# The layout of three bf16 parts that a gather by matmul reads, in a mixture-of-experts kernel

## The chip, the cores and the metric

One core of one Trainium2 chip runs the whole program. The metric is the device time of one execution in microseconds (us); lower is better. The time before is the median of 3 runs, 1986.92 us (1986.51 to 1989.77). One further execution was profiled; all rows come from it.

## What is computed

A two-part encoder layer on 256 tokens of 2048 channels, in float32. The first part (token mixing with four branches) and the modulation vectors are not touched by the change. The second part is the one that matters:

```python
h2 = modulate(rmsnorm(x, norm2_g[l]), sh2, sc2)     # norm, then * (1 + scale) + shift per channel
pg = softmax(ht @ rg_w + rg_b); pg_top, g_idx = top_k(pg, 1)          # 1 group of 4
le = (ht @ re_w + re_b)[group]; pe_top, e_idx = top_k(softmax(le), 2) # 2 of its 8 experts
y = (silu(x_tok @ w1[e]) * (x_tok @ w3[e])) @ w2[e]  # for each token's two experts of 32
x = x + gt2 * sum_of_weighted(y);  out = rmsnorm(x, final_g)
```

Each expert has 12 MB of float32 weights (w1, w3, w2), and all 32 of them are read once.

## The kernel before

The program has one instruction stream for each engine, synchronised by counting semaphores that are written out by hand.

**The normalised input and its parts.** After the token mixing, `xn2` (in the buffer `r_b`, 128 partitions x 4096 elements, that is 2 tiles of 128 tokens with 2048 channels each) holds the normalised rows. TensorE transposes them (line 715) for the router. For the experts they are kept as three bf16 parts whose sum is the float32 value, in `xparts` (line 145): ScalarE rounds `xn2` to part 0 (line 1020), GpSimd subtracts part 0 from it in place (line 470, first instruction, which also waits until the transposes have read `r_b`), ScalarE rounds the remainder to part 1 (line 1032), and GpSimd subtracts again and writes part 2 (line 470, second instruction). All four write and read their elements in the order of memory. In ScalarE's stream line 1032 stands behind the two exponentials of the router (lines 1028 and 1030).

**The router** runs at the same time: logits on TensorE (lines 723 and 724), then a chain of small VectorE instructions (lines 1368 to 1459), each waiting for the one before, with a few matmuls between them. It ends in a table that says which expert each pass takes, and in one-hot selection matrices: `sel` (bf16, who goes where) and `selw` (with weights). `sel_e` is the piece of 64 columns for one pass.

**The pass loop.** A pass computes one expert for up to 64 tokens. `gather(half)` (line 758) builds the input of a pass, transposed: for each of 8 blocks of 128 channels it adds up six matmuls (2 token tiles x 3 parts), in which a 128-column piece of `xparts` is the stationary operand and the 64 columns of `sel_e` are the moving one; 48 matmuls in all. A channel block k is the set of channels q*16 + k, since the expert weights are loaded with 16 neighbouring channels in one partition. So the stationary operand takes every 16th bf16 element (`xparts_k`, line 146), a step of 32 bytes. VectorE scales and shifts the result (lines 1481 and 1484) into `xe`. `first(p)` (line 802) multiplies `xe` with w1 and w3, four channel blocks (one chunk c) at a time; `second` (line 780) multiplies with w2. The loads of a pass are issued by SyncE (lines 411 and 417), each when TensorE has finished with the buffer (`w13_used`, `w2_used`); there are buffers for one expert. Before the loop, `gather(0)` and `gather(1)` of pass 0 stand alone (lines 823 to 825), then come the transposes of `selw` (line 830) and `first(0)`; within `first(p)` stands `gather(0)` of the next pass, behind chunk 1, and `gather(1)` stands between `first(p-1)` and `first(p)`.

**Waits around the parts.** The gather waits for both subtractions (`parts_sub`, line 822); VectorE waits for them before it writes `selw` into `r_b` (lines 1461 and 1462). SyncE issues no load of the loop before the table is there (line 431).

Of the kernel before, what the change touches and what calls it, by code (L numbers as in the profile page):

```python
# [14 lines left out]
ALU = mybir.AluOpType  # L15
ACT = mybir.ActivationFunctionType
AX_X = mybir.AxisListType.X

P = 128
D = 2048  # L20
S = 256
KT = D // P
TT = S // P
# [44 lines left out]
def build(nc, x, c, ada_w, ada_b, norm1_g, w_in, pool_w, pool_scale, conf_dw_w, conf_dw_b, conf_ln_g,  # L68
          conf_ln_b, branch_w, sc_conv_w, w_o, norm2_g, rg_w, rg_b, re_w, re_b, exp_w1, exp_w3,
          exp_w2, final_g, keep_consts, mix_consts, iota_const, out):  # L70
    with ExitStack() as ctx:
        def sb(name, shape, dt=F32):
            return ctx.enter_context(nc.sbuf_tensor(name, shape, dt))

        def sem(name):
            return ctx.enter_context(nc.semaphore(name))
# [5 lines left out]
        r_b = sb("r_b", [P, KT * S])  # L82
# [17 lines left out]
        xn2 = r_b[:, :].rearrange("p (t d) -> p t d", t=TT)  # L100
# [22 lines left out]
        def at(name, shape, dt, offset):  # L123
            return nc.alloc_sbuf_tensor_at(name, shape, dt, offset=base + offset)
# [18 lines left out]
        xe = ring[:, 5, 0:KT * NWIN].rearrange("p (c n) -> p c n", c=KT)  # L143
        y_sb = ring[:, 5, 1024:2048].rearrange("p (b n) -> p b n", b=2)
        xparts = at("xparts", [P, 3, TT, D], BF16, 90112)
        xparts_k = xparts[:, :, :, :].rearrange("p i t (q k) -> p i t k q", k=KT)
        sel = r_c[:, 0:576].bitcast(BF16).rearrange("p (t j) -> p t j", t=TT)
        sel_e = r_c[:, 576:640].bitcast(BF16).rearrange("p (t n) -> p t n", t=TT)
        wT = r_c[:, 640:1664].rearrange("p (i t) -> p i t", i=4)
# [3 lines left out]
        selw = r_b[:, 1024:3072]  # L153
        fgrow = r_b[:, 2048:4096]
        squares = r_b[:, 0:2048]
        remain = r_b
        ident, ones, tri = keep[:, 0:128], keep[:, 128:256], keep[:, 256:384]
        io8 = keep[:, 384:400].rearrange("p (t e) -> p t e", t=TT)
        prow = ring[:, 0, 0:384].rearrange("p (a b) -> p a b", a=3)
# [20 lines left out]
        def tiles(b, n=2):  # L180

            return ps[:, b:b + n, :].rearrange("p b (h t) -> p (b h) t", t=S)
# [51 lines left out]
        h2_t = sem("h2_t")  # L234
# [30 lines left out]
        parts_sub = sem("parts_sub")  # L265
        parts_act = sem("parts_act")
# [37 lines left out]
        def y_bank(n):  # L304
            return 4 * (n % 2) + 2
# [154 lines left out]
        @block.gpsimd  # L460
        def _(pool):
            pool.dma_start(r_c[:, :], mix_consts).then_inc(mixc_in, 16)

            flat = "p t d -> p (t d)"
            for i in range(2):
                pool.wait_ge(parts_act, i + 1)
                dst = remain[:, :] if i == 0 else xparts[:, 2, :, :].rearrange(flat)
                if i == 0:
                    pool.wait_ge(h2_t, 8)
                nc.gpsimd.tensor_tensor(dst, r_b[:, :], xparts[:, i, :, :].rearrange(flat),  # L470
                                        ALU.subtract).then_inc(parts_sub, 1)


        @block.tensor
        def _(pe):
            mm = nc.tensor.matmul
# [12 lines left out]
            for b in range(8):  # L489
                for k in (2 * b, 2 * b + 1):  # L490
                    for t in range(TT):
                        last = nc.tensor.transpose(tiles(b, 1)[:, k % 2, t * P:(t + 1) * P],
                                                   x_in[:, t, k * P:(k + 1) * P], ident)
# [47 lines left out]
            for n in range(5):  # L541
# [3 lines left out]
                if n == 3:  # L545

                    pe.wait_ge(conv_done, 1)
                    for m in range(MT):
                        last = mm(ps[:, y_bank(n), 0:S], ones, brT[:, 1, m, :], start=(m == 0), stop=(m == MT - 1))
                    last.then_inc(ln_sum, 1)  # L550
                if n == 4:
                    pe.wait_ge(ln_step, 1)
                    pe.wait_ge(sc_done, 1)
                    for m in range(MT):
                        last = mm(ps[:, y_bank(n), 0:S], ones, pq[:, m, 0:S], start=(m == 0), stop=(m == MT - 1))
# [11 lines left out]
            for q in range(4):  # L567
                b = (2, 3, 6, 7)[q]
                for t in range(TT):
                    last = mm(ps[:, b, :], tmp[0][:, t * MIX + q * P:t * MIX + (q + 1) * P], dftp[:, t, :],  # L570
                              start=(t == 0), stop=(t == TT - 1))
# [4 lines left out]
            for q in range(4):  # L576
                for t in range(TT):
                    last = mm(pt[:, q, :], tmp[1][:, t * MIX + q * P:t * MIX + (q + 1) * P], pool_c[:, t, q, :],
                              start=(t == 0), stop=(t == TT - 1))
            last.then_inc(pool_done, 1)  # L580

            def gate_y(n, kts, lhs, rhs):

                y = tiles(y_bank(n))
                for f in range(4):
                    for k in range(kts):
                        last = mm(y[:, f, :], lhs(k, f), rhs(k), start=(k == 0), stop=(k == kts - 1))  # L587
                return last
# [3 lines left out]
            for q in range(4):  # L592
                mm(tiles(2)[:, q, :], dftc[:, 0:128], pq[:, q, 0:S], start=True, stop=False)
                last = mm(tiles(2)[:, q, :], dftc[:, 128:256], pq[:, q, S:2 * S], start=False, stop=True)
# [26 lines left out]
            for j in range(4):  # L621
# [15 lines left out]
                last = gate_y(n, 1, lambda k, f: pw[:, j, f * P:(f + 1) * P], lambda k: brT[:, 0, j, :])  # L637
# [3 lines left out]
            for k in range(KT):  # L641
                last = mm(ps[:, 6, k:k + 1], acc_k[:, k, :], ones[:, 0:1], start=True, stop=True)
# [28 lines left out]
            for k in range(KT):  # L671
                last = mm(ps[:, 6, k:k + 1], acc[:, k * P:(k + 1) * P], ones[:, 0:1], start=True, stop=True)
# [7 lines left out]
            def wo_products(k, t, n):  # L680
                y = 2 * k + n // 2
                hi = g_hi[y % 4][:, (n % 2) * MIX:(n % 2 + 1) * MIX]
                o = (y % 4) * 1024 + (n % 2) * MIX
                lo = g_lo[:, (WO0 + y // 4) % W_SLOTS, o:o + MIX]
                m_hi = (m_hi_a, m_hi_b)[k // 8][:, k % 8, t * P:(t + 1) * P]
                mm(ps[:, 4 * t + n, :], m_hi, hi, start=(k == 0), stop=False)  # L686
                mm(ps[:, 4 * t + n, :], m_hi, lo, start=False, stop=False)  # L687
                return mm(ps[:, 4 * t + n, :], m_lo[:, k, t * P:(t + 1) * P], hi, start=False, stop=(k == KT - 1))  # L688

            for y in range(28):  # L690
# [3 lines left out]
                for t in (1, 0):  # L694
# [3 lines left out]
                    for n in (2 * (y % 2), 2 * (y % 2) + 1):  # L698
                        last = wo_products(y // 2, t, n)
                last.then_inc(g_used, 1)  # L700
            pe.wait_ge(g_lo_done, 128 + 32)
            for t in range(TT):
                for n in range(4):
                    for k in (14, 15):
                        last = wo_products(k, t, n)
# [6 lines left out]
            for b in range(8):  # L712
                for k in (2 * b, 2 * b + 1):
                    for t in range(TT):
                        last = nc.tensor.transpose(tiles(b, 1)[:, k % 2, t * P:(t + 1) * P],
                                                   xn2_k[:, t, k, :], ident)
# [10 lines left out]
            for t in range(TT):  # L727
                last = nc.tensor.transpose(ps[:, 1, t * 36:(t + 1) * 36], logitT[:, t * P:(t + 1) * P],
                                           ident[0:36, 0:36])
# [21 lines left out]
            gat = ps[:, 0, :].rearrange("p (c n) -> p c n", n=NWIN)  # L751

            def gather(half):
                for kk in range(HALF):
                    k = half * HALF + kk
                    for t in range(TT):
                        for i in range(3):
                            last = mm(gat[:, kk, :], xparts_k[:, i, t, k, :], sel_e[:, t, :],  # L758
                                      start=(t == 0 and i == 0), stop=(t == TT - 1 and i == 2))
                last.then_inc(gathered, 1)  # L760

# [31 lines left out]
            def first(p, with_second):  # L793
                for c in range(4):
                    if c % 2 == 0:
                        pe.wait_ge(xe_ready, 2 * p + c // 2 + 1)
                    for m in range(2):
                        pe.wait_ge(w13_in[2 * c + m], 16 * p + 16)
                    for kk in range(4):
                        k = 4 * c + kk  # L800
                        for m in range(2):
                            last = mm(ps[m * NWIN:(m + 1) * NWIN, 2, :], xe[:, k, :],  # L802
                                      chunk(2 * c + m)[:, kk * F:(kk + 1) * F],
                                      start=(k == 0), stop=(k == KT - 1))
                    last.then_inc(w13_used, 1)
                    if with_second and c == 0:
                        second(p, 0, 2)
                    if c == 1:
                        pe.wait_ge(sel_ready, p + 2)
                        pe.wait_ge(xe_ready, 2 * p + 2)  # L810
                        gather(0)
                        if with_second:
                            second(p, 2, 4)
                    if with_second and c == 2:
                        for b in range(2):
                            turn_output(p, b)
# [11 lines left out]
            for i in range(4):  # L828
                for t in range(TT):
                    last = nc.tensor.transpose(tiles(4)[:, i, t * P:(t + 1) * P],  # L830
                                               selw[:, t * PAIRS + i * P:t * PAIRS + (i + 1) * P], ident)
# [16 lines left out]
            for i in range(4):  # L848
# [6 lines left out]
                for k in range(KT):  # L855
                    last = nc.tensor.transpose(ps[:, b + k // 4, (k % 4) * P:(k % 4 + 1) * P],
                                               YS[:, k, i * P:(i + 1) * P], ident)
                last.then_inc(yT_done, 1)
            yn = ring[:, 0:2, :].rearrange("p s (i d) -> p (s i) d", d=D)
            for t in range(TT):  # L860
# [5 lines left out]
                for n in range(4):  # L866
                    for i in range(4):
                        last = mm(ps[:, 4 * t + n, :], wT[:, i, t * P:(t + 1) * P], yn[:, i, n * MIX:(n + 1) * MIX],  # L868
                                  start=(i == 0), stop=(i == 3))
# [4 lines left out]
        def _(act):  # L874
            A = nc.scalar.activation
# [21 lines left out]
            for t in range(TT):  # L897
                last = A(r_b[:, t * D:(t + 1) * D], x_in[:, t, :], ACT.Square, accum_out=stat[:, t:t + 1])
# [118 lines left out]

            act.wait_ge(xn2_ready, 2)
            act.wait_ge(x1_ready, 8)
            A(xparts[:, 0, :, :], xn2, ACT.Copy).then_inc(parts_act, 1)  # L1020
            for b in range(0, 8, 2):
                act.wait_ge(h2_t, b + 1)
                for k in (2 * b, 2 * b + 1):
# [5 lines left out]
            act.wait_ge(r_ask, 2)  # L1029
            A(rs[:, 8, :], rs[:, 7, :], ACT.Exp).then_inc(r_exp, 1)  # L1030
            act.wait_ge(parts_sub, 1)
            A(xparts[:, 1, :, :].rearrange("p t d -> p (t d)"), remain[:, :], ACT.Copy).then_inc(parts_act, 1)
            act.wait_ge(table_ready, 1)
            A(sel_e, sel[:, :, 0:NWIN], ACT.Copy).then_inc(sel_ready, 1)  # L1034
            act.wait_ge(selw_t, 1)
# [578 lines left out]
```

## Time and profile before

| | |
|---|---|
| median of 3 runs | 1986.92 us |
| the profiled execution's own time | 1989.88 us |
| its span, first to last instruction | 1988.1 us (1.8 us less than its time) |
| mean granted clock of TensorE | 0.951 of full |
| busy: TensorE matmul, VectorE, ScalarE, GpSimd | 91%, 37%, 21%, 1% of the span |
| instructions of the gather (line 758) | 3120 matmuls, 65 gathers of 48 |

The busy times of TensorE are modelled ends of pipelined matmuls, so the distance from one start to the next is the better measure of its pace. The profile gives for each stretch the granted clock (1.00 is 2.4 GHz, 0.50 is 1.2 GHz), the share of time in which the 16 DMA engines are busy, and the rate that they move. All positions are microseconds from the start of the span.

### The profile page before, as it was taken

How to read it: one execution, taken by the hardware profiler on the slowest of the kernel's cores; microseconds unless marked ns; L12 is line 12 of the kernel's file. 1: busy time of each engine (PE TensorE's matmuls, PEld its weight loads, DVE VectorE, ACT ScalarE, POOL GpSimd, SP SyncE). 2: the span in 40 equal slices, each digit the busy share in tenths (PEclk: the TensorE clock that was granted, in tenths of full speed). 3: DMA queues.
4: the chain of work that ended last, by engine and by line, in shares of the span. 5: the costliest groups of instructions: out<-in, count | busy, mean ns of one | idle time of the engine just before them, and what ended most of it. 6: DMA issues, size and time to landing. Idle time of an engine off the chain costs nothing.

```text
span 1988.1 us, 28852 instructions
## 1 busy us (share of the span) xinstructions
PE 1815.1 (91%) x11742; PEld 1233.8 (62%) x11742; DVE 729.1 (37%) x824; ACT 424.3 (21%) x506; POOL 16.8 (1%) x7
## 2 busy tenths in 40 slices
PE   1189999999999999997399999999999999999987
PEld 1178855998999999886245454544545445445444
DVE  5848855585545634444611111111111111111113
ACT  3020003332323323334111111111111111111112
POOL 0000000000000000000300000000000000000000
PEclk8589999998999999998699999999999999999999
DMA  8998676497565644455099999999999999999971
GB/s 364 419 367 329 239 294 250 156 399 292 218 249 206 259 170 170 160 194 208 5 380 422 422 422 422 422 422 422 422 422 422 422 422 422 422 422 422 422 333 64
DMA packets 128765, 641.11 MB, mean 322 GB/s; under 512 B 12944, under 2 KB 13380, under 8 KB 64196
## 3 DMA queue, kind: packets, MB, share of 16 engines
q1 hardware_dynamic: 127568, 638.12, 79.4%
q0 software_dynamic: 144, 1.70, 0.2%
q8 instruction: 46, 0.75, 0.1%
q10 hardware_dynamic: 996, 0.44, 0.1%
q14 instruction: 11, 0.09, 0.0%
HBM read 638.14 MB, written 2.10 MB: 322 GB/s over the span
## 4 chain that ended last, share of the span: by engine, by line
PE 70%; DMA 21%; DVE 6%; issue 1%; ACT 1%; ACTq 0%; SPq 0%; DVEq 0%
DMA ring<-in_exp_w 17%; PE ps L802 16%; PE ps L523 7%; PE ps L780 7%; PE ps L758 6%; PE ps L611 5%; PE ps L613 5%; PE ps L615 5%; PE ps L587 4%; DMA ring<-in_ada_w 4%; PE ps L536 3%; DVE r_m L1119 2%; PE ps L868 1%; PE ps L686 1%; PE ps L687 1%; PE ps L688 1%
## 5 line engine op out<-in xcount | busy, mean ns | idle before, releaser
L802 PE MATMUL ps<-ring 128*64 128x512 f32 x2048 | 468.1, 599 | 8.4 <-DMA ring<-in_exp_w 5.0
L802 PEld LDWEIGHTS ps<-ring 128*64 128x64 f32 x2048 | 151.1, 137 | 270.9 <-issue 265.7
L615 PE MATMUL ps<-h_hi,g_lo 128*128 128x256 f32 x1024 | 293.6, 287 | 0.0
L1481 DVE TENSOR_TENSOR r_c<-ps,scale 128x512 f32<-128x512 f32 x65 | 44.9, 691 | 535.4 <-PE ps L758 535.2
L758 PEld LDWEIGHTS ps<-r_c,xparts 128*128 128x128 bf16 x3120 | 199.6, 168 | 58.6 <-issue 51.1
L611 PE MATMUL ps<-h_hi,mix_hi 128*128 128x256 f32 x768 | 224.5, 292 | 6.8 <-DVE g_lo L1242 3.7
L613 PE MATMUL ps<-h_lo,mix_hi 128*128 128x256 f32 x768 | 221.3, 288 | 0.0
L758 PE MATMUL ps<-r_c,xparts 128*128 128x64 bf16 x3120 | 206.6, 228 | 7.3 <-ACT r_c L1034 5.2
L615 PEld LDWEIGHTS ps<-h_hi,g_lo 128*128 128x128 f32 x1024 | 200.6, 196 | 0.0
L975 ACT ACTIVATE mix_hi<-ring 128x1024 fp32r<-128x1024 f32 x96 | 101.3, 1059 | 276.1 <-PE ps L615 263.4
L611 PEld LDWEIGHTS ps<-h_hi,mix_hi 128*128 128x128 f32 x768 | 151.8, 198 | 8.2 <-DVE g_lo L1242 4.3
L1119 DVE SCALAR_TENSOR_TENSOR r_m<-ring,ccol,r_m 128x2048 f32<-128x2048 f32 x60 | 141.1, 2352 | 39.5 <-DMA ring<-in_ada_w 37.9
L1242 DVE TENSOR_TENSOR g_lo<-ring,mix_hi 128x1024 fp32r<-128x1024 f32 x96 | 117.2, 1225 | 98.8 <-ACT mix_hi L975 96.3
L613 PEld LDWEIGHTS ps<-h_lo,mix_hi 128*128 128x128 f32 x768 | 151.7, 198 | 0.4
L523 PE MATMUL ps<-r_h,ring 128*128 128x256 f32 x640 | 140.4, 383 | 1.4 <-ACT r_h L913 1.4
L1059 ACT ACTIVATE ring<-ps 128x512 f32<-128x512 f32 x64 | 34.7, 595 | 471.5 <-PE ps L780 471.5
L523 PEld LDWEIGHTS ps<-r_h,ring 128*128 128x128 f32 x640 | 122.9, 192 | 18.4 <-issue 1.4
L780 PE MATMUL ps<-ring,r_c 128*64 128x512 f32 x512 | 119.2, 607 | 3.1 <-DVE r_c L1498 3.1
L780 PE MATMUL ps<-r_b,r_c 128*64 128x512 f32 x512 | 116.9, 598 | 0.0
L1490 DVE TENSOR_TENSOR r_m<-ps,mod 128x512 f32 x64 | 41.2, 687 | 203.0 <-PE ps L790 203.0
L587 PE MATMUL ps<-r_b,ring 128*128 (+1 forms) x416 | 94.3, 384 | 0.3 <-DVE mod L1156 0.3
L780 PEld LDWEIGHTS ps<-ring,r_c 128*64 128x64 f32 x512 | 40.8, 139 | 79.9 <-issue 79.9
(247 smaller groups left out, 1675.4 us busy)
## 6 DMA issues: line engine op xcount, KB each, us to landing
ring<-in_exp_w SPq DMA_DIRECT2D x320, 1024.0 KB, 21.1
ring<-in_w_in SPq DMA_DIRECT2D x46, 2048.0 KB, 8.9
ring<-in_ada_w SPq DMA_DIRECT2D x32, 2048.0 KB, 11.8
r_b<-in_exp_w SPq DMA_DIRECT2D x64, 1024.0 KB, 21.2
ring<-in_ada_w SPq DMA_DIRECT2D x32, 1024.0 KB, 9.0
ring<-in_w_o SPq DMA_DIRECT2D x8, 2048.0 KB, 7.6
ring<-in_branch_w SPq DMA_DIRECT2D x6, 2048.0 KB, 10.7
r_m<-in_x SPq DMA_DIRECT2D x1, 2048.0 KB, 12.9
```

Source lines behind the costliest of these rows:

```text
L523: last = mm(u[:, f, :], w[:, kk, f * P:(f + 1) * P], hT[:, k, :], start=(k == 0 and f % 2 == 0), stop=(k == KT - 1), skip_group_check=True)
L536: last = mm(ps[:, u_bank(n) + t, :], hT[:, k, t * P:(t + 1) * P], w[:, kk, :], start=(k == 0), stop=(k == KT - 1))
L587: last = mm(y[:, f, :], lhs(k, f), rhs(k), start=(k == 0), stop=(k == kts - 1))
L611: mm(u[:, f, :], hi[:, o:o + P], h_hi[:, k, :], start=(k == 0 and f % 2 == 0), stop=False, skip_group_check=True)
L613: mm(u[:, f, :], hi[:, o:o + P], h_lo[:, k, :], start=False, stop=False, skip_group_check=True)
L615: last = mm(u[:, f, :], lo[:, o:o + P], h_hi[:, k, :], start=False, stop=(k == KT - 1), skip_group_check=True)
L758: last = mm(gat[:, kk, :], xparts_k[:, i, t, k, :], sel_e[:, t, :], start=(t == 0 and i == 0), stop=(t == TT - 1 and i == 2))
L780: last = mm(ps[side * NWIN:(side + 1) * NWIN, 4 + b, :], hid[:, f, :], chunk(CHUNKS + f)[:, q * MIX:(q + 1) * MIX], start=(f == 0), stop=( ...
L802: last = mm(ps[m * NWIN:(m + 1) * NWIN, 2, :], xe[:, k, :], chunk(2 * c + m)[:, kk * F:(kk + 1) * F], start=(k == 0), stop=(k == KT - 1))
L975: A(g_hi[x % 4], slot(q % W_SLOTS)[:, (x % 4) * 1024:(x % 4 + 1) * 1024], ACT.Copy).then_inc(g_hi_done, 1)
L1119: ins = V.scalar_tensor_tensor(out=acc, in0=w[:, i, :], scalar=ccol[:, kk:kk + 1], in1=acc, op0=ALU.mult, op1=ALU.add)
L1242: V.tensor_tensor(g_lo[:, q, (x % 4) * 1024:(x % 4 + 1) * 1024], slot(q)[:, (x % 4) * 1024:(x % 4 + 1) * 1024], g_hi[x % 4].bitcast(F32), ...
```

## The change

`xparts` is kept contraction-major: within each token tile, channel q*16 + k is stored at k*128 + q. The four instructions that make the parts walk `r_b` in the order of memory, as before, and walk `xparts` with an inner step of 128 elements (256 bytes) and 16 steps, for each of 128 channels q. The gather reads 128 neighbouring elements. Nothing else is changed; number, order, waits and sizes of all instructions stay. The values computed are the same.

```diff
-        xparts_k = xparts[:, :, :, :].rearrange("p i t (q k) -> p i t k q", k=KT)
+        xparts_q = xparts[:, :, :, :].rearrange("p i t (k q) -> p i t q k", k=KT)
+        xn2_q = r_b[:, :].rearrange("p (t q k) -> p t q k", t=TT, k=KT)
...
-            flat = "p t d -> p (t d)"
-            for i in range(2):
-                pool.wait_ge(parts_act, i + 1)
-                dst = remain[:, :] if i == 0 else xparts[:, 2, :, :].rearrange(flat)
-                if i == 0:
-                    pool.wait_ge(h2_t, 8)
-                nc.gpsimd.tensor_tensor(dst, r_b[:, :], xparts[:, i, :, :].rearrange(flat),
-                                        ALU.subtract).then_inc(parts_sub, 1)
+            pool.wait_ge(parts_act, 1)
+            pool.wait_ge(h2_t, 8)
+            nc.gpsimd.tensor_tensor(xn2_q, xn2_q, xparts_q[:, 0, :, :, :], ALU.subtract).then_inc(parts_sub, 1)
+            pool.wait_ge(parts_act, 2)
+            nc.gpsimd.tensor_tensor(xparts_q[:, 2, :, :, :], xn2_q, xparts_q[:, 1, :, :, :], ALU.subtract
+                                    ).then_inc(parts_sub, 1)
...
-                            last = mm(gat[:, kk, :], xparts_k[:, i, t, k, :], sel_e[:, t, :],
+                            last = mm(gat[:, kk, :], xparts[:, i, t, k * P:(k + 1) * P], sel_e[:, t, :],
...
-            A(xparts[:, 0, :, :], xn2, ACT.Copy).then_inc(parts_act, 1)
+            A(xparts_q[:, 0, :, :, :], xn2_q, ACT.Copy).then_inc(parts_act, 1)
...
-            A(xparts[:, 1, :, :].rearrange("p t d -> p (t d)"), remain[:, :], ACT.Copy).then_inc(parts_act, 1)
+            A(xparts_q[:, 1, :, :, :], xn2_q, ACT.Copy).then_inc(parts_act, 1)
```

## Rows read from the trace of the kernel before

**Rows 1.** Windows: busy time of each engine, TensorE's clock, DMA share, GB/s.
```profile
core 0: us, PE busy (x) PEld busy (x) DVE busy (x) ACT busy (x) POOL busy (x), PEclk, DMA share, GB/s
980.00:985.00 5.00, 3.23 (x48) 3.10 (x48) 4.48 (x9) 0.31 (x1) 0.00 (x0) 0.50 0.01 3
...
994.00:1000.00 6.00, 6.00 (x16) 2.01 (x18) 0.00 (x0) 0.00 (x0) 0.00 (x0) 0.52 0.73 309
...
1012.00:1014.00 2.00, 2.00 (x10) 0.43 (x6) 0.00 (x0) 0.00 (x0) 0.00 (x0) 1.00 0.91 303
...
1022.00:1024.00 2.00, 2.00 (x12) 0.79 (x10) 0.00 (x0) 0.00 (x0) 0.00 (x0) 1.00 0.95 299
...
1024.00:1100.00 76.00, 76.00 (x530) 37.39 (x528) 11.62 (x18) 10.97 (x16) 0.00 (x0) 1.00 1.01 422
...
1500.00:1925.00 425.00, 418.38 (x2896) 206.47 (x2892) 64.00 (x100) 70.32 (x101) 0.00 (x0) 1.00 1.01 422
```
**Rows 2.** The chain that ended last: start, length, what.
```profile
944.04 7.03 PE ps L723 x32
...
961.84 6.81 DVE ct L1412
...
1057.40 3.15 PE ps L758 x48
...
1086.46 3.12 PE ps L758 x48
...
1791.14 25.43 DMA ring<-in_exp_w
...
1820.96 25.43 DMA ring<-in_exp_w
```
**Rows 3.** Timeline of the parts and the router: start, length, instruction, idle before.
```profile
938.83 3.62 ACT L1020 ACTIVATE xparts<-r_b 128x4096 bf16<-128x4096 f32 x1
...
944.20 7.94 POOL L470 TENSOR_TENSOR r_b<-r_b,xparts 128x4096 f32<-128x4096 f32 x1 [942.28 <-PE ps L715]
...
952.93 0.17 DVE L1372 TENSOR_TENSOR r<-lg,rs 128x8 f32<-128x8 f32 x1
...
956.95 3.60 ACT L1032 ACTIVATE xparts<-r_b 128x4096 bf16<-128x4096 f32 x1
...
960.63 7.93 POOL L470 TENSOR_TENSOR xparts<-r_b,xparts 128x4096 bf16<-128x4096 f32 x1 [8.49 <-ACT xparts L1032]
...
961.84 6.80 DVE L1412 TENSOR_SCALAR ct<-ct 32x128 f32<-32x128 f32 x1
```
**Rows 4.** Timeline between the table and the loop.
```profile
981.65 3.23 PE L758 MATMUL ps<-r_c,xparts 128*128 128x64 bf16 x48 [5.25 <-ACT r_c L1034]
...
985.43 0.69 DVE L1481 TENSOR_TENSOR r_c<-ps,scale 128x512 f32<-128x512 f32 x1 [0.26 <-DVE r_b L1468]
...
986.91 3.21 PE L758 MATMUL ps<-r_c,xparts 128*128 128x64 bf16 x48 [2.03 <-DVE ring L1484]
...
993.99 9.92 PE L802 MATMUL ps<-ring 128*64 128x512 f32 x32 [2.12 <-issue]
...
1000.66 21.68 SPq L411 DMA_DIRECT2D ring<-in_exp_w  x10
...
1014.02 3.18 PE L758 MATMUL ps<-r_c,xparts 128*128 128x64 bf16 x48
```
**Rows 5.** Line 758: duration in ns (least, median, most), first and last start.
```profile
L758 PE MATMUL ps<-r_c,xparts x3120: 225/227/274, 981.6 to 1912.7; 128*128 128x64 bf16 x195
```
**Rows 6.** Line 503 alone (128x128 f32 weights, one column): windows, neighbouring, then strided.
```profile
core 0: us, PE busy (x) PEld busy (x), PEclk, DMA share, GB/s
259.00:262.00 3.00, 3.00 (x29) 3.00 (x28) 1.00 1.01 374
361.00:364.00 3.00, 3.00 (x15) 3.00 (x15) 1.00 0.00 0
```

More of the change, by code:

```diff
@@ L155, in build @@
         squares = r_b[:, 0:2048]
-        remain = r_b
         ident, ones, tri = keep[:, 0:128], keep[:, 128:256], keep[:, 256:384]
```

## Prediction

> **What bounds the kernel now.** I read the windows first. From 1024 us to 1925 us the sixteen DMA engines are fully busy and move 422 GB/s in every stretch [rows 1]; this is the reading of the expert weights. Then the chain that ended last. In its first half it runs through TensorE alone, and one gather of the same kind follows the other after 1086.46 - 1057.40 = 29.06 us [rows 2]. In its second half it is a transfer of 25.43 us, once in 1820.96 - 1791.14 = 29.82 us [rows 2]. 12 MB (12.58 million bytes) at 422 GB/s are 29.8 us, so the pass is bound by the DMA, and TensorE, which could do a pass in 29.06 us, only catches up over some sixteen passes and then waits. Since the DMA is full from 1024 us on in both halves, the end of the loop is set by the moment at which the stream of loads starts again and by the bytes, not by TensorE.
>
> So the stretch that matters lies before. The DMA stands still while the router makes its table (0.01 busy at 980 to 985 us, [rows 1]); SyncE may not go on without it. The first load of the loop that waits for TensorE goes out at 1000.66 us [rows 4]. Everything on the way from the normalised rows to that point moves the end one for one. The reader is to see two things on that way. One is an instruction of VectorE on 32x128 elements that takes 6.80 us and stands in the chain that ended last [rows 2, 3]. It starts at 961.84 us, while GpSimd's second subtraction runs from 960.63 us for 7.93 us, to 968.56 us; VectorE's instruction ends at 968.64 us, 0.08 us later [rows 3]. The next starts of the router follow from there. VectorE was held until GpSimd was done. The other is the gather of pass 0, twice, at 981.65 and 986.91 us [rows 4].
>
> **The change part by part.** It moves no wait and adds no instruction; it changes how the same elements lie, and so only durations.
>
> The gather. 65 x 48 matmuls read their stationary operand as neighbours instead of with a step of 32 bytes. Before, 48 of them take 3.18 us at the full clock [rows 4], less 0.23 us for the last one's own length [rows 5], over 47: 63 ns from start to start. At half the clock it is (3.23 - 0.25) / 47 = 63 ns as well [rows 1, 4]. In the loop a saving is hidden: the DMA's 29.82 us stand against 29.06 us. Should it be halved there, TensorE waits 3 us more in each pass. It can show only before 1024 us. The first gather of pass 0 ends at 984.88 us, but the VectorE instruction that reads it starts at 985.43 us, behind VectorE's own work on `selw` [rows 4], so it is worth nothing. The second (986.91 us) is on the path, and two short gaps of the DMA, at 1012 to 1014 and 1022 to 1024 us, stand behind gathers: 2 x (1 - 303/422) = 0.56 us and 2 x (1 - 299/422) = 0.58 us [rows 1].
>
> What the new pace is, no row says; the bounds are these. The one like case is the float32 column sum of line 503, in one stretch with neighbouring and in another with strided weights, both at the full clock: 29 against 15 matmuls in 3 us, 103 against 200 ns, a ratio of 1.93 [rows 6]. By it the gather's pace would fall to 33 ns at the full clock, and at 1.2 GHz to no less than the 53 ns that 64 columns take. The other bound is no change, because 63 ns at both clocks looks like a pace that isn't set in the array. I take no change, 0 us. The rows alone don't decide that, since a strided read may be blind to the clock too. The other end is 47 x 10 ns = 0.5 us in the second gather plus 1.1 us of gaps, 1.6 us gained; and if the second gather cost nothing at all, 3.2 + 1.1 = 4.3 us. The Trainium skill ("TensorE: Matmul & The Clock Gate", section "Wait — 56ns, not 53.3ns?") says that the sequencer needs about 62 ns for each matmul where its hardware decoder is off. The trace agrees with 63 ns, whatever the clock, and by that rule the layout of the weights gains nothing here.
>
> ScalarE's two roundings (3.62 and 3.60 us, [rows 3]) read as before and write with a step of 256 bytes. No row shows a strided write to the on-chip memory. 4096 elements in 3.6 us are one in 0.88 ns; I take them unchanged, since their reads are. As the other bound serves the ratio 1.93: 3.4 us more each. The second lies wholly on the path (GpSimd's second subtraction waits for it). Of the first about 3 us would come through, because ScalarE's share of the transposes is queued behind it and the logits, which start at 944.04 us [rows 2], wait for those.
>
> GpSimd's two subtractions take 7.94 and 7.93 us with everything in order [rows 3]. Now one of the two inputs is read with a step of 256 bytes, and the second also writes so. The bounds are x1 (nothing changes; below that nothing, as no access gets simpler) and x1.93 for all of it [rows 6]. I take half of the surcharge, because one of two inputs is strided: x1.465, 11.6 us each, 3.7 us more. Where does it land? The first would then end at 944.20 + 11.63 = 955.83 us. In that time VectorE starts the router: its first instruction with two inputs in the on-chip memory is line 1372 at 952.93 us [rows 3]. If it is held as line 1412 was, the whole chain of the router, all queued behind it, starts 955.83 - 952.93 = 2.9 us later; before, the first subtraction was over 0.79 us ahead of it. ScalarE's second rounding stands behind the router's exponentials and moves along; so does the second subtraction. This one is 3.7 us longer, and line 1412 waits it out. Sum: 2.9 + 3.7 = 6.6 us. If neither changes, 0; if both are x1.93 (15.3 us), 6.6 + 7.4 = 14.0 us; with ScalarE's too, 19 us. The Trainium skill ("GPSIMD Engine Reference", section "Performance pitfalls for Q7 kernels") gives about 2.9 instead of 1.9 cycles per element when a read's step is over 8 bytes. No run here shows it yet; by it, x1.5, the sum would be 3.2 + 4.0 = 7.2 us.
>
> The clock adds an uncertainty. `first(0)` runs at half the clock until about 1000 us (0.52 in 994 to 1000 us, [rows 1]); when everything is later, the clock may rise a little earlier or later in it. I give that 1.5 us to both sides and no term.
>
> The sum against the profiled execution: 1989.88 + 6.6 = 1996.5 us. That execution was 3 us above the median of the runs, so for the median 1986.92 + 6.6 = 1993.5 us.
>
> **The rivals.** (1) GpSimd isn't slowed. For it: its 1.94 ns per element is already more than twice ScalarE's, so the access may not be what it waits for. Against it: both kinds of strided read that can be compared differ by 1.93. The time is then 1986.9 us, or with the faster gather 1986.9 - 1.6 = 1985.3 us. This is the case on the other side: not slower. It decides as long as the two subtractions together grow by less than about 4.8 us (0.8 us of slack, then 4 us for 0.2%). (2) The gather is bound by its reads and falls to 33 ns, and GpSimd is slowed as forecast: 6.6 - 1.6, 1991.9 us. (3) GpSimd is slowed, but VectorE's small instructions of two inputs are not held by the first subtraction; only the second counts: +3.7, 1990.6 us. For it: before, none of them fell into GpSimd's time. Against it: line 1412, with one input, was held. The Trainium skill ("SBUF — State Buffer", section "Who interferes with whom") says that such instructions do wait for a GpSimd instruction that reads. (4) The strided writes cost too, in GpSimd or ScalarE: +14 to +19, 2001 to 2006 us. (5) That the gathers gain in every pass would need a loop bound by TensorE; rows 1 speak against it.
>
> **How the numbers follow.** Forecast (with case 2, which is near it) 0.45; case 1 with or without a faster gather 0.26; case 3 0.11; case 4 0.15; anything that makes it faster by over 4 us 0.03. The range runs from case 1 with the faster gather, 1984.8 us, to the middle of case 4, 2003 us. Less than 0.2% (4 us) is about what a measurement can't tell from no change. Slower by more: the forecast and case 4, 0.60; within it: cases 1 and 3, 0.37; faster: 0.03.
>
> **What would show it.** In the trace of the changed kernel: the two subtractions at 11 to 12 us; line 1372 starting when the first one ends, after 955 us; line 1412 ending within 0.1 us of the second; the gather at 63 ns per matmul; the first load of the loop that waits for TensorE near 1007 us instead of 1000.66 us; from some 20 us later to the end 422 GB/s, and a distance from there to the end as before. The prediction is wrong if the subtractions stay at 7.9 us, if ScalarE's roundings grow, or if the loads show gaps in the loop.

## The result: 22 us slower, and the profile after

The changed kernel takes 2010.7 us (median of 4 runs, 2009.8 to 2014.3) against 1988.3 us for the kernel before in the same comparison: a ratio of 1.0114, 95% interval 1.0099 to 1.0130, that is 20 to 26 us slower. Its profiled execution took 2014.28 us, its span is 2012.5 us.

The timeline of the changed kernel, around the parts and the router (start, length, engine, line, instruction, idle time before it and what ended it). Its line numbers are two to four lower than those of the kernel before: 1018 and 1030 are ScalarE's roundings, 466 and 468 GpSimd's subtractions, 1370 the router's first instruction with two inputs, 1410 the one that was held, 756 the gather.

```profile
938.47 18.79 ACT L1018 ACTIVATE xparts<-r_b 128x4096 bf16<-128x4096 f32 x1
...
956.75 3.89 ACT L1022 ACTIVATE r_m<-ps,mod,scale 128x256 f32<-128x256 f32 x8
957.34 10.86 POOL L466 TENSOR_TENSOR r_b<-r_b,xparts 128x4096 f32<-128x4096 f32 x1 [955.43 <-ACT xparts L1018]
958.05 8.95 PE L721 MATMUL ps<-r_m 128*36 128x256 f32 x32 [14.36 <-ACT r_m L1022]
...
968.87 0.17 DVE L1370 TENSOR_TENSOR r<-lg,rs 128x8 f32<-128x8 f32 x1
...
972.87 18.40 ACT L1030 ACTIVATE xparts<-r_b 128x4096 bf16<-128x4096 f32 x1
...
977.75 0.21 DVE L1410 TENSOR_SCALAR ct<-ct 32x128 f32<-32x128 f32 x1
...
990.78 0.59 ACT L1032 ACTIVATE r_c<-r_c 128x128 bf16<-128x128 bf16 x1
991.35 18.43 POOL L468 TENSOR_TENSOR xparts<-r_b,xparts 128x4096 bf16<-128x4096 f32 x1 [23.15 <-ACT xparts L1030]
...
1009.92 2.72 PE L756 MATMUL ps<-r_c,xparts 128*128 128x64 bf16 x48 [24.18 <-POOL xparts L468]
...
1027.69 18.42 SPq L411 DMA_DIRECT2D ring<-in_exp_w  x10
```

Read beside [rows 3, 4] it shows the loss in two places. The first rounding takes 18.79 us instead of 3.62 us, and ScalarE's share of the transposes stands behind it; so TensorE waits 14.36 us with the logits, and does them in 8.95 us instead of 7.03 us [rows 2]. Counted from the start of the first rounding, the router's first instruction with two inputs comes after 30.4 us instead of 14.1 us [rows 3]: 16.3 us. Of these, 14.4 us pass before the logits start (958.05 - 938.47 = 19.6 us against 5.1 us before), and 1.9 us are the slower logits. After its pause TensorE stands at half the clock in some 3 us of them, where before it had the full clock throughout (1.00 from 944 to 951 us). Two windows of the changed kernel (columns as in [rows 1]):

```profile
960.00:961.00 1.00, 1.00 (x3) 0.37 (x2) 0.00 (x0) 0.98 (x3) 1.00 (x1) 0.50 0.00 0
...
962.00:963.00 1.00, 1.00 (x7) 0.50 (x5) 0.00 (x0) 0.00 (x0) 1.00 (x1) 1.00 0.00 0
```

The second place is behind the router. The second rounding takes 18.40 us, the second subtraction 18.43 us, in a row, and the gather waits for them, 24.18 us idle: from the second rounding's start to the first gather it is 1009.92 - 972.87 = 37.1 us instead of 24.7 us [rows 3, 4], 12.4 us more. By then the table has been ready for 19 us (ScalarE's `sel_e`, line 1032, at 990.78 us). In return the 6.6 us in which line 1412 was held are gone (line 1410, 0.21 us). They gain nothing, since the table isn't what is waited for any more.

The gather got faster, at full clock more than twice, and the loop doesn't care. From start to start a matmul takes (2.72 - 0.24) / 47 = 53 ns at half the clock, and at full clock (1.57 - 0.19) / 47 = 29 ns, against 63 ns before at both (the timeline's 1.57 us stands below, the 0.19 us are the one matmul's length). A window of the changed kernel in the loop (columns as in [rows 1]):

```profile
1100.00:1500.00 400.00, 362.68 (x2764) 156.34 (x2762) 60.86 (x95) 65.34 (x93) 0.00 (x0) 0.98 1.01 422
```

And its chain that ended last, two steps of it (start, length, what):

```profile
1786.54 25.43 DMA ring<-in_exp_w
...
1816.35 25.43 DMA ring<-in_exp_w
```

422 GB/s and 29.81 us for a pass, as before [rows 1, 2]; the 3.2 us that TensorE saves in each pass became waiting (362.68 us busy of 400, before all of it), and its mean granted clock in that window is 0.98 instead of 1.00.

### The profile page after: what moved, and what is told of

The parts are those of the page before. It is cut to its first block, busy times and chain, and to the rows that moved or that the text cites. A ratio compares the mean times of both kernels' runs of the same rounds, so it can differ in the third digit from the quotient of the medians.

```text
span 2012.5 us, 28852 instructions
## 1 busy us (share of the span) xinstructions
PE 1738.0 (86%) x11742; PEld 1139.1 (57%) x11742; DVE 722.4 (36%) x824; ACT 453.8 (23%) x506; POOL 30.2 (1%) x7
## 4 chain that ended last, share of the span: by engine, by line
PE 51%; DMA 38%; DVE 5%; issue 2%; ACT 2%; POOLq 1%; SPq 1%; POOL 1%; ACTq 0%; DVEq 0%
DMA ring<-in_exp_w 33%; PE ps L800 9%; PE ps L521 7%; PE ps L609 5%; PE ps L611 5%; PE ps L613 5%; PE ps L585 4%; DMA ring<-in_ada_w 4%; PE ps L534 3%; DVE r_m L1117 2%; PE ps L778 2%; PE ps L866 1%; PE ps L684 1%; PE ps L686 1%; PE ps L685 1%
## 5 line engine op out<-in xcount | busy, mean ns | idle before, releaser
L800 PE MATMUL ps<-ring 128*64 128x512 f32 x2048 | 486.3, 618 | 82.7 <-DMA ring<-in_exp_w 80.4
L800 PEld LDWEIGHTS ps<-ring 128*64 128x64 f32 x2048 | 159.3, 141 | 361.2 <-issue 357.4
L756 PEld LDWEIGHTS ps<-r_c,xparts 128*128 128x128 bf16 x3120 | 96.0, 99 | 78.7 <-issue 75.8
L521 PEld LDWEIGHTS ps<-r_h,ring 128*128 128x128 f32 x640 | 122.8, 192 | 18.4 <-issue 1.4
L756 PE MATMUL ps<-r_c,xparts 128*128 128x64 bf16 x3120 | 103.7, 194 | 26.9 <-POOL xparts L468 24.2
L501 PE MATMUL ps<-keep,r_m 128*128 128x1 f32 x128 | 24.5, 326 | 71.5 <-DVE r_m L1117 71.5
## 6 DMA issues: line engine op xcount, KB each, us to landing
ring<-in_branch_w SPq DMA_DIRECT2D x6, 2048.0 KB, 10.9
```

The costliest lines, as they stand in the source:

```text
L521: last = mm(u[:, f, :], w[:, kk, f * P:(f + 1) * P], hT[:, k, :], start=(k == 0 and f % 2 == 0), stop=(k == KT - 1), skip_group_check=True)
L756: last = mm(gat[:, kk, :], xparts[:, i, t, k * P:(k + 1) * P], sel_e[:, t, :], start=(t == 0 and i == 0), stop=(t == TT - 1 and i == 2))
L800: last = mm(ps[m * NWIN:(m + 1) * NWIN, 2, :], xe[:, k, :], chunk(2 * c + m)[:, kk * F:(kk + 1) * F], start=(k == 0), stop=(k == KT - 1))
```

## The experiments

The execution before this stretch varies by some microseconds from run to run, so beside the ratios I count in each profile from the start of the first rounding: to the first gather, and to the end of the span. The column after these is their difference, the way from the first gather to the end.

| kernel | first rounding to first gather, us | to the end, us | first gather to the end, us | ratio to before (95% interval) |
|---|---|---|---|---|
| before | 42.8 | 1049.3 | 1006.5 | 1 |
| changed | 71.5 | 1074.0 | 1002.6 | 1.0114 (1.0099 to 1.0130) |
| e1_read_only | 44.2 | 1046.3 | 1002.1 | 0.9986 (0.9976 to 0.9997) |
| e2_write_only | 71.2 | 1076.9 | 1005.7 | 1.0138 (1.0118 to 1.0158) |
| e3_turn_on_read | 45.8 | 1048.4 | 1002.6 | 0.9997 (0.9988 to 1.0007) |
| e4_turn_in_f32 | 42.9 | 1045.5 | 1002.5 | 0.9986 (0.9977 to 0.9995) |
| e5_vector_subtracts | 38.2 | 1040.1 | 1002.0 | 0.9962 (0.9948 to 0.9975) |
| e6_first_part | 59.1 | 1062.7 | 1003.6 | 1.0081 (1.0061 to 1.0100) |
| e7_other_parts | 55.3 | 1057.2 | 1001.9 | 1.0058 (1.0041 to 1.0075) |

**The two halves of the change, each alone.** e1 is the kernel before with

```diff
-                            last = mm(gat[:, kk, :], xparts_k[:, i, t, k, :], sel_e[:, t, :],
+                            last = mm(gat[:, kk, :], xparts[:, i, t, k * P:(k + 1) * P], sel_e[:, t, :],
```

> The kernel before with one edit: the gather reads 128 neighbouring columns of parts that lie as before. It leaves out the right order of channels, so the experts get permuted inputs; the work is the same. Theory W (the strided writes alone cost the time, the neighbouring reads gain a little): the gather at 53 ns per matmul at half the clock and 29 ns at full, as in the changed kernel; time 2 to 4 us under the kernel before (1.4 us from the second gather before the loop, 1.1 us from two gaps of the DMA). Rival G (the faster gather lets TensorE idle in the loop and drop its clock, and that costs at the end): 0 to 5 us over the kernel before.

and e2 is the changed kernel with that line the other way round.

> The changed kernel with one edit: the gather reads with a step of 16 columns again, so its input is in the wrong order of channels; the work is the same. Theory W: the four instructions that make the parts take 18.8, 10.9, 18.4 and 18.4 us as in the changed kernel, the gather 63 ns per matmul, and the time is that of the kernel before plus about 26 us (the gather of the changed kernel began 28.3 us later, less 1 to 2 us that lie in waits of the DMA). Rival G: plus 22 us or less, as in the changed kernel, since the loop then keeps its clock.

e1 is 2.8 us faster (0.14%), e2 27.4 us slower (1.38%); both came as theory W says, and the halves add up to the change (27.4 - 2.8 = 24.6, measured 22.7 with an interval of 20 to 26). Rival G is out: in e1 the mean granted clock falls to 0.942 (before 0.951, changed kernel 0.939), and the time is still lower. The timeline of e1 has the neighbouring reads at both clocks:

```profile
985.21 2.74 PE L758 MATMUL ps<-r_c,xparts 128*128 128x64 bf16 x48 [5.25 <-ACT r_c L1034]
...
1002.48 18.43 SPq L411 DMA_DIRECT2D ring<-in_exp_w  x10
1005.67 1.57 PE L758 MATMUL ps<-r_c,xparts 128*128 128x64 bf16 x48
```

What is the faster gather worth? The column "first gather to the end" answers it in one way: with all three parts in neighbours the way from the first gather to the end takes 1002.0 to 1002.6 us, with none 1005.7 and 1006.5 us, so 3 to 4.5 us less. These are one profile each; the ratios of e1 and e4 give 2.8 us, with intervals from 0.6 or 1.0 to 4.8 or 4.6 us. In e1 it isn't seen whole in the time to the end (3.0 us), because its first gather came 1.4 us late for a reason that isn't in the edit: the transposes of the profiled execution ran at half the clock (0.50 from 941 to 946 us; in the kernel before 0.72 over its own). First e1's row, then that of the kernel before:

```profile
941.12 6.48 PE L715 MATMUL ps<-keep,r_b 128*128 128x128 f32 x32 [9.31 <-ACT r_b L1016]
...
938.94 5.10 PE L715 MATMUL ps<-keep,r_b 128*128 128x128 f32 x32 [9.31 <-ACT r_b L1016]
```

Two pieces of the gain can be named. In the 30 us after the first load that waits for TensorE, e1's DMA engines move 399 GB/s, those of the kernel before 383 GB/s. That is 16 x 30 / 422 = 1.1 us, as the two gaps of [rows 1] said; 0.5 us is the second gather itself (3.21 us [rows 4] against 2.74 us). The rest was not taken apart. TensorE's clock rises earlier in e1's `first(0)`, which takes 8.78 us instead of 9.92 us [rows 4], but that isn't the gather's doing: e2, with the strided gather, takes 8.78 us for it too, and the changed kernel, with the fast one, 9.87 us.

**What a strided access costs, by itself.** The probe is the kernel before with rows of instructions of 4096 elements behind its end, such as

```python
A(slot(4)[:, 0:2048].bitcast(BF16).rearrange("p (k q) -> p q k", q=128), slot(3).rearrange("p (q k) -> p q k", q=128), ACT.Copy)
```

> The kernel before, and behind its end a row of copies of 4096 elements on ScalarE and VectorE and subtractions on GpSimd, each alone, with one side strided: bf16 writes with steps of 2, 4, 8, 16 and 128 elements, float32 writes with 2, 4, 16 and 128, float32 reads with 4, 16 and 128, bf16 reads with 128. Theory W: reads on ScalarE stay at 3.6 us; a bf16 write with 128 takes 18 us on ScalarE and GpSimd alike, and either every step over 1 does, or only those over some width that the row shows; float32 writes are not or less slow. Rival R: strided reads are as slow as strided writes. Then five subtractions in order on GpSimd (7.9 us each), and in each one small instruction of VectorE: two inputs (tensor_tensor, scalar_tensor_tensor), a reduction, and tensor_scalar of 32x128 and 128x2. If two inputs share what GpSimd reads through, the first two and the 32x128 one last until the subtraction ends (about 5 us); if only line 1412's kind is held, only that one does. The time grows by some 250 us through the rows added.

The probe takes 2159.5 us in its one execution, 171 us more, all behind the end of the kernel's own work. Its expectation says "each alone"; that isn't quite what ran. Each engine's rows follow one another, but the rows of ScalarE run beside those of VectorE and then of GpSimd. The changed kernel has the same bf16 writes, on ScalarE while GpSimd stands still and on GpSimd while ScalarE does, and they take the same time (18.79, 18.40 and 18.43 us), so it isn't the neighbour that makes them slow. ScalarE's timeline follows. Lines 1127 to 1137 write bf16 with steps of 1, 2, 4, 8, 16 and 128 elements; 1139 to 1147 write float32 with 1, 2, 4, 16 and 128; 1149 to 1153 read float32 with 4, 16 and 128, and 1155 reads bf16 with 128.

```profile
1986.11 3.62 ACT L1127 ACTIVATE ring<-ring 128x4096 bf16<-128x4096 f32 x1 [6.33 <-DMA out<-ring]
1989.76 4.75 ACT L1129 ACTIVATE ring<-ring 128x4096 bf16<-128x4096 f32 x1
1994.53 9.51 ACT L1131 ACTIVATE ring<-ring 128x4096 bf16<-128x4096 f32 x1
2004.08 18.98 ACT L1133 ACTIVATE ring<-ring 128x4096 bf16<-128x4096 f32 x1
...
2040.62 18.47 ACT L1137 ACTIVATE ring<-ring 128x4096 bf16<-128x4096 f32 x1
2059.13 3.62 ACT L1139 ACTIVATE ring<-ring 128x4096 f32<-128x4096 f32 x1
2062.78 3.90 ACT L1141 ACTIVATE ring<-ring 128x4096 f32<-128x4096 f32 x1
2066.71 7.61 ACT L1143 ACTIVATE ring<-ring 128x4096 f32<-128x4096 f32 x1
...
2081.58 7.27 ACT L1147 ACTIVATE ring<-ring 128x4096 f32<-128x4096 f32 x1
2088.89 7.59 ACT L1149 ACTIVATE ring<-ring 128x4096 f32<-128x4096 f32 x1
...
2111.38 7.40 ACT L1155 ACTIVATE ring<-xparts 128x4096 f32<-128x4096 bf16 x1
```

GpSimd's timeline in the probe: 478 all in order; 480 and 484 write bf16 and float32 with a step of 128; 486 reads the bf16 input and 492 the float32 input with 128.

```profile
2022.94 7.96 POOL L478 TENSOR_TENSOR ring<-ring,xparts 128x4096 bf16<-128x4096 f32 x1 [1054.21 <-DVE r_m L1632]
2030.98 18.44 POOL L480 TENSOR_TENSOR ring<-ring,xparts 128x4096 bf16<-128x4096 f32 x1
...
2068.10 8.01 POOL L484 TENSOR_TENSOR ring<-ring,xparts 128x4096 f32<-128x4096 f32 x1
2076.18 10.95 POOL L486 TENSOR_TENSOR ring<-ring,xparts 128x4096 bf16<-128x4096 f32 x1
...
2106.51 10.45 POOL L492 TENSOR_TENSOR ring<-ring,xparts 128x4096 bf16<-128x4096 f32 x1
```

So a bf16 write costs by its step: on ScalarE 1.3 times at 4 bytes, 2.6 times at 8 bytes, and 4.8 to 5.2 times from 16 bytes on (18.98 us at 16 bytes, 17.51 us at 32, 18.47 us at 256), some 4.5 ns an element; on GpSimd the same 4.5 ns. Why it is this much no run shows. A float32 write costs ScalarE twice from 16 bytes on, and GpSimd nothing at its one step, 512 bytes. A strided read from 16 bytes on costs ScalarE twice, whatever the type, and GpSimd at 256 and 512 bytes 2.5 to 3.0 us, 1.3 to 1.4 times. The first subtraction of the changed kernel (10.86 us, strided read, float32 write) and the second (18.43 us, bf16 write) are these rows again. Theory W is borne out for GpSimd and only half for ScalarE, whose reads I expected to stay at 3.6 us; rival R is wrong where it matters, since the writes of 2 bytes stand alone.

The second part of the probe has five subtractions in order on GpSimd (7.93 us each) and, in each, one small instruction of VectorE:

```profile
2119.32 5.68 DVE L1636 TENSOR_TENSOR r_m<-r_m 128x8 f32<-128x8 f32 x1
...
2127.34 5.77 DVE L1640 SCALAR_TENSOR_TENSOR r_m<-r_m 128x16 f32<-128x16 f32 x1
...
2135.44 0.17 DVE L1644 TENSOR_REDUCE r_m<-r_m 128x2 f32<-128x16 f32 x1
...
2143.54 5.72 DVE L1648 TENSOR_SCALAR r_m<-r_m 32x128 f32<-32x128 f32 x1
...
2151.55 5.82 DVE L1652 TENSOR_SCALAR r_m<-r_m 128x2 f32<-128x2 f32 x1
```

Four of five last until the subtraction is over (the first runs from 2117.04 for 7.94 us, to 2124.98 us, the instruction of VectorE to 2125.00 us); the reduction isn't held. Instructions of VectorE with two inputs (128x8 and 128x16) are held as well as `tensor_scalar` (32x128 and 128x2). This term of my prediction was right, but it didn't come to bear: in the changed kernel the router's first instruction with two inputs starts at 968.87 us, after the first subtraction's end at 968.20 us.

**Do the losses add up?** e6 writes only part 0 contraction-major and e7 only parts 1 and 2, each with the changed kernel's strided writes; the gather reads each part as it lies:

```diff
-                            last = mm(gat[:, kk, :], xparts_k[:, i, t, k, :], sel_e[:, t, :],
+                            last = mm(gat[:, kk, :], (xparts[:, i, t, k * P:(k + 1) * P] if i == 0 else xparts_k[:, i, t, k, :]), sel_e[:, t, :],
```

(e7 has the two forms the other way round.)

> Only part 0 is contraction-major, by the changed kernel's strided write; parts 1 and 2 lie and are read as before. Theory W, with the two places of the loss: ScalarE's 18.8 us delay the router (its first instruction with two inputs some 15.9 us later than before, counted from the start of the first rounding), and nothing else; the second subtraction takes 7.9 us and holds line 1412 for 6.8 us again. Time: 15.9 us over before, less about 1 us for the 16 faster matmuls of each gather, 14 to 16 us. Rival (the two strided roundings share one cost, so that either alone costs most of the 22 us): over 18 us.

> Only parts 1 and 2 are contraction-major, by strided writes; part 0 lies and is read as before. Theory W: the first rounding 3.6 us, the first subtraction 7.9 us, then 18.4 us and 18.4 us; the router isn't delayed, line 1412 isn't held (0.2 us) because the second subtraction starts only when it is over, and the first gather starts 12.3 us later than before, counted from the start of the first rounding. Time: 12.3 us over before less about 2 us, 9 to 12 us; with e6_first_part it adds up to the loss of the changed kernel. Rival: as for e6_first_part, over 18 us.

Up to the first gather e6 loses 16.3 us and e7 12.5 us, 28.8 us together; the changed kernel loses 28.6 us. There the losses add up. In the whole times this is only seen roughly: by the ratios it is 16 us (12 to 20) and 12 us (8 to 15), 28 us together, against 22.7 us (20 to 26) of the changed kernel. In e6 the router is late and the second subtraction holds its line 1412 again; in e7 the router is in time, nothing holds line 1413, and the gather waits 24 us. The timeline of e6:

```profile
939.33 18.80 ACT L1020 ACTIVATE xparts<-r_b 128x4096 bf16<-128x4096 f32 x1
...
977.40 7.93 POOL L470 TENSOR_TENSOR xparts<-r_b,xparts 128x4096 bf16<-128x4096 f32 x1 [8.32 <-ACT xparts L1032]
978.60 6.80 DVE L1412 TENSOR_SCALAR ct<-ct 32x128 f32<-32x128 f32 x1
```

The timeline of e7 (its lines are one higher):

```profile
957.39 0.21 DVE L1413 TENSOR_SCALAR ct<-ct 32x128 f32<-32x128 f32 x1
...
971.00 18.43 POOL L471 TENSOR_TENSOR xparts<-r_b,xparts 128x4096 bf16<-128x4096 f32 x1 [23.30 <-ACT xparts L1033]
...
989.57 2.76 PE L759 MATMUL ps<-r_c,xparts 128*128 128x64 bf16 x48 [24.19 <-POOL xparts L471]
```

Both expectations hold, e6's at the upper edge of its 14 to 16 us. The rival, a cost that either alone would bring (over 18 us), doesn't fit: up to the first gather each shows its own part and no more. The whole time of e6 alone, up to 20 us, would not rule it out.

**The same layout without the strided writes.** e3 changes the order where the float32 rows are read:

```diff
-            A(xparts[:, 0, :, :], xn2, ACT.Copy).then_inc(parts_act, 1)
+            A(xparts_q[:, 0, :, :, :], xn2_k, ACT.Copy).then_inc(parts_act, 1)
...
+            nc.gpsimd.tensor_tensor(rem_q, xn2_k, xparts_q[:, 0, :, :, :], ALU.subtract).then_inc(parts_sub, 1)
```

> The same contraction-major parts, but the order is changed where the float32 rows are read: ScalarE reads them with a step of 64 bytes and writes part 0 in the order of memory, GpSimd reads them so too and writes the remainder, in the new order, to a free buffer; everything behind that is in the order of memory. Theory W (a strided write of 2 bytes costs 4.5 ns per element, a strided read little): ScalarE 3.6 and 3.6 us, GpSimd 10 to 12 and 7.9 us; time 0 to 4 us under the kernel before. Rival R (what costs is a walk in short runs of 16 elements, on either side): ScalarE's first at 18 us, GpSimd's first at 11 us or more, time at least 12 us over the kernel before. If VectorE's router instructions with two inputs are held by GpSimd's first subtraction, line 1372 or its like starts only when that ends.

It is as fast as before (0.9997), at the edge of what theory W gave. ScalarE's first rounding takes 7.14 us, and ScalarE's share of the transposes stands behind it, so the first gather comes 3.0 us later and the gather's gain is spent. GpSimd's first subtraction takes 9.97 us, but it ends at 953.97 us, just as the router's first instruction with two inputs starts (953.89 us), and holds nothing up. I had expected 3.6 us for the rounding; rival R expected 18 us.

e4 changes the order where the rows say that it costs nothing: in GpSimd's float32 write, and in a second rounding of part 0 at a time when ScalarE is idle. The gather waits for that one too.

```diff
+            nc.gpsimd.tensor_tensor(rem.rearrange("p (t k q) -> p t q k", t=TT, k=KT), xn2_q,
+                                    p0.rearrange("p (t q k) -> p t q k", t=TT, k=KT),
+                                    ALU.subtract).then_inc(parts_sub, 1)
...
+            A(xparts[:, 1, :, :].rearrange("p t d -> p (t d)"), rem, ACT.Copy).then_inc(parts_act, 1)
+            A(xparts_q[:, 0, :, :, :], xn2_k, ACT.Copy).then_inc(parts_act, 1)
```

> The contraction-major parts, with the order changed only where the rows measured so far say that it is free or hidden. ScalarE rounds part 0 in the order of memory into a scratch buffer (3.6 us); GpSimd reads in order and writes the float32 remainder with a step of 512 bytes to a free buffer (8.01 us alone, against 7.96 in order); part 1 and part 2 are then made in order; ScalarE makes the contraction-major part 0 behind part 1, reading with a step of 64 bytes (7.3 us), where it is idle until the table. Theory W: nothing of this is on the path, so the time is that of the run that only changed the read, about 3 us (0.14%) under the kernel before. Rival: GpSimd's float32 write is slower when VectorE and TensorE work beside it, over 8.8 us, and then holds line 1372: 0 to 2 us under.

The timeline of e4, the two instructions that change the order:

```profile
937.14 8.00 POOL L468 TENSOR_TENSOR r_m<-r_b,ring 128x4096 f32<-128x4096 f32 x1 [935.23 <-ACT ring L1023]
...
955.14 7.10 ACT L1036 ACTIVATE xparts<-r_b 128x4096 bf16<-128x4096 f32 x1
```

0.9986 (0.9977 to 0.9995): 2.8 us faster, just what the reads alone gave in e1, and theory W's forecast. Line 1412's instruction (here line 1416) is held for 6.83 us as before. So the layout is worth about 0.14%, if its making is hidden.

e5 goes after the 6.8 us of line 1412, which no version so far has touched: VectorE makes part 2 itself, in four pieces in its own pauses.

```diff
+                return V.tensor_tensor(xparts[:, 2, j // 2, s], rem[:, j * 1024:(j + 1) * 1024],
+                                       xparts[:, 1, j // 2, s], ALU.subtract)
```

> As e4_turn_in_f32, and the second subtraction goes to VectorE in four pieces of 1024 columns (1.2 us each by line 1242's rows), two while VectorE waits for the position matmuls, one while it waits for the start matmuls, one behind the table. Theory L (line 1412 is held only by GpSimd's second subtraction, as the probe's rows say for every instruction that it held): line 1412 takes 0.2 us, the table is ready 4 to 5.5 us earlier, and the time is 4 to 5.5 us under e4_turn_in_f32, 7 to 8.5 us (0.35 to 0.43%) under the kernel before. Rival: the pieces themselves stand in the chain of the router, 4.8 us in all, so the gain over e4_turn_in_f32 is under 2.5 us.

The timeline of e5; line 1416 is a piece of the subtraction, line 1424 the one that was held:

```profile
957.03 2.48 DVE L1416 TENSOR_TENSOR xparts<-r_m,xparts 128x1024 bf16<-128x1024 f32 x2
...
959.86 0.21 DVE L1424 TENSOR_SCALAR ct<-ct 32x128 f32<-32x128 f32 x1
960.63 1.21 DVE L1416 TENSOR_TENSOR xparts<-r_m,xparts 128x1024 bf16<-128x1024 f32 x1
...
973.01 1.23 DVE L1416 TENSOR_TENSOR xparts<-r_m,xparts 128x1024 bf16<-128x1024 f32 x1 [0.23 <-DVE r_c L1472]
```

The gather comes 38.2 us after the first rounding instead of 42.9 us, 4.8 us earlier, and the kernel takes 0.9962 of the time before: 7.6 us less, 1979.7 us. Theory L holds: line 1424 isn't held, and by the ratios the gain over e4 is 4.8 us, where the rival gave under 2.5 us. This version beats both kernels, and more than half of its gain is not the layout's. No run took the hold away in the kernel before, so that this part comes without the layout as well is argued, not shown.

## Why the prediction was wrong

I forecast 1993.5 us (+6.6) and a range up to 2003.0 us; it was 2010.7 us. Rival 4, that the strided writes cost too, had the mechanism; I gave it 0.15 and 14 to 19 us, and it came to 22.7 us. (The range's lower end was written as 1984.8 us; by the rival it comes from it is 1985.3 us.) Point by point:

- **Where the time is decided: right.** DMA-bound loop, 422 GB/s, 29.8 us for a pass; a delay before the loop moves the end one for one. All the runs bear that out: e2's first gather is 28.4 us late and its end 27.6 us.
- **ScalarE's two roundings, "I take them unchanged, since their reads are": this step failed.** 18.8 and 18.4 us instead of 3.6. I had no row of a strided write and put in its place the ratio of a strided read on another engine, 1.93, as the upper bound. The write of 2 bytes costs 5.2 times. A bound borrowed from another direction, type and engine was none. With the measured lengths in it, my own working would have gone wrong the other way. The first rounding is 15.2 us longer and delays the logits by 14.4 us, much as I had it (3 of 3.4 us); the half clock behind TensorE's pause adds 1.9 us, for which I had no term. Together they are the 16.3 us of e6. The second rounding and subtraction are 14.8 + 10.5 = 25.3 us longer, and I had both wholly on the path; they cost 12.4 us. Before, 13.1 us lay between the end of the second subtraction (968.56 us) and the first gather (981.65 us), in which the router finished its table [rows 3, 4]; now the gather starts 0.14 us behind the subtraction. 25.30 - 13.09 + 0.14 = 12.35 us, the 12.4 us of the second place.
- **GpSimd's subtractions: the first one near, the second mis-sized.** 10.9 us for the first, forecast 11.6, from half the surcharge of a TensorE row, which was in part luck. The second 18.4 us, since it writes bf16; forecast 11.6, bound 15.3. The Trainium skill's read rule ("GPSIMD Engine Reference", section "Performance pitfalls for Q7 kernels", half as much again for a wide step) is close to the trace: 7.96 to 10.95 us and 10.45 us, 1.3 to 1.4 times. The loss was not in the read but in the write.
- **VectorE held by GpSimd: the mechanism is right, the term fell away.** The probe shows it for two inputs, but the router came so late that the first subtraction was over, and the instruction of line 1412 (here line 1410) was not held at all. The way that sets the end changed from the table to the parts, which I didn't foresee because I let none of the four instructions be long enough.
- **The gather "I take no change": wrong.** 63 ns at both clocks was not the pace of issue but that of the strided read; 29.4 ns now at the full clock. The rule of the Trainium skill that I leaned on ("TensorE: Matmul & The Clock Gate", section "Wait — 56ns, not 53.3ns?") gives 62 ns for a matmul only where the hardware decoder is off. That I took this to be so here was unfounded: in e1 the matmuls follow each other at 29.4 ns with nothing but their layout changed, so the 62 ns don't bind, and the agreement with 63 ns was chance. The row that did tell was the strided float32 case of [rows 6]: ratio 1.93 there, 2.2 here. The other half of that step stands: the gain in the whole kernel is small (2.8 us by the ratio, 3 to 4.5 us by the profiles; I had 1.6 for this case) because the loop hides it.

## What to carry to other kernels

A new layout has to be written by someone: before judging what the reader gains, measure or look for a row of the write with that step and that element size, on that engine. Where the order must be changed, do it in a float32 write on GpSimd or in a read, and off the path, not in a 2-byte write with 16 bytes or more between elements. And ask of each instruction of GpSimd which small instructions of VectorE it holds; taking that away, on top of the new layout, gave more here (4.8 us) than the layout (2.8 us).

## What the runs showed of the hardware that I had not expected

- A bf16 write with a step of 16 bytes or more takes some 4.5 ns an element (4.3 to 4.6) on ScalarE and on GpSimd alike, against 0.88 and 1.94 ns in order. On VectorE a copy from float32 to bf16 goes from 2.29 us to 9.31 us for 4096 elements, 2.3 ns an element.
- GpSimd's float32 write is free at a step of 512 bytes (8.01 against 7.96 us); ScalarE's costs twice (7.27 us).
- TensorE's stationary bf16 operand, 128 columns for 64 of the moving one: a matmul each 63 ns with a step of 32 bytes and 29.4 ns with neighbours at full clock; at half clock 53 ns, as many cycles of 1.2 GHz as there are columns (64). In mixed gathers at full clock the mean is near what each matmul's own price gives: with one part of three in neighbours (e6) 51 to 52 ns, by the two prices 52; with two (e7) 41 ns, by the prices 41. At half the clock that isn't so: with one of three, 48 took 2.75 us, with two (e7) 2.76 us, with all (e1) 2.74 us, with none 3.23 us [rows 4]; why is open.
